# Holding back the first weight loads of the second block until a late row gather has landed

## Time and profile before

| | us |
|---|---|
| runs, not profiled | 2386.42, 2394.18, 2394.52; median 2394.18 |
| profiled execution, its own time | 2388.13 |
| its span | 2386.2 |
| PE, DVE, ACT, POOL busy | 1805.4, 1295.7, 840.0, 653.5 |
| moved by DMA | 933.05 MB, 391 GB/s over the span |

### The profile page before, as it was taken

One profiled execution on the slowest core, in us unless ns is written; L12 is line 12 of the kernel. 1 busy time (PEld: TensorE's weight loads), 2 busy tenths in 40 slices (PEclk: granted clock), 3 DMA queues, 4 the chain that ended last, 5 costly groups with the idle time before them and its releaser, 6 DMA issues.

```text
span 2386.2 us, 30584 instructions
## 1 busy us (share of the span) xinstructions
PE 1805.4 (76%) x11098; PEld 848.8 (36%) x11098; DVE 1295.7 (54%) x3184; ACT 840.0 (35%) x2262; POOL 653.5 (27%) x604
## 2 busy tenths in 40 slices
PE   6999777686787777687779557777669996766676
PEld 3654612151252343153336113333336552222222
DVE  4868777668746766856876867455424321111111
ACT  1224354434445544444744435333323410000000
POOL 1002244434433433433443444333320300000000
PEclk9999876696698888689979678877879988787878
DMA  9984999999999999999999999999986369999999
GB/s 393 376 344 194 369 422 421 421 420 420 403 421 421 420 421 420 419 390 420 420 416 421 421 420 421 421 418 419 422 328 238 140 274 428 428 428 429 428 429 378
DMA packets 110284, 933.05 MB, mean 391 GB/s; under 512 B 12710, under 2 KB 14020, under 8 KB 16644
## 3 DMA queue, kind: packets, MB, share of 16 engines
q0 software_dynamic: 76800, 549.70, 56.0%
q1 hardware_dynamic: 33348, 381.60, 38.6%
HBM read 930.15 MB, written 6.06 MB: 392 GB/s over the span
## 4 chain that ended last, share of the span: by engine, by line
DMA 50%; PE 31%; DVE 9%; ACT 6%; issue 3%; POOL 1%; SPq 0%; DVEq 0%; POOLq 0%
DMA arena<-in_peer_uv_dram,arena 28%; DMA arena<-in_moe_pieces_dram 15%; PE summed L1354 6%; DVE y_g L2781 4%; DMA mod<-in_w_parts_dram 4%; PE gp L962 3%; PE gp L1427 3%; PE gp L981 2%; DMA arena<-in_w_parts_dram 2%; PE gp L1717 2%; PE gp L972 2%; PE gp L1423 1%; PE gp L1556 1%; ACT arena L2054 1%; DMA arena<-in_w_slots_dram 1%
## 5 line engine op out<-in xcount | busy, mean ns | idle before, releaser
L1354 PE MATMUL summed<-arena 64*64 64x512 f32 x4096 | 694.6, 777 | 360.5 <-ACT arena L2054 336.5
L2781 DVE CUSTOM_DVE_ANT_0 y_g<-arena,h 128x1024 f32<-128x1024 f32 x512 | 627.1, 1225 | 459.5 <-DMA arena<-in_peer_uv_dram,arena 386.6
L902 POOL DMA_INDIRECT arena<-in_peer_uv_dram,arena x512 | 589.7, 1152 | 926.7 <-PE summed L1354 825.9
L1354 PEld LDWEIGHTS summed<-arena 64*64 64x64 f32 x4096 | 133.7, 157 | 796.8 <-ACT arena L2054 704.4
L2048 ACT ACTIVATE arena<-arena 128x1 f32<-128x1 f32 x512 | 102.7, 201 | 602.1 <-DVE arena L2781 601.4
L1717 PE MATMUL gp<-arena,mod 128*32 128x512 f32 x1008 | 164.3, 788 | 105.1 <-DMA arena<-in_moe_pieces_dram 105.1
L2054 ACT ACTIVATE arena<-cst,arena 128x128 f32<-128x128 f32 x512 | 205.5, 401 | 16.7
L3164 DVE TENSOR_TENSOR mod<-mod,gp 128x512 f32<-128x512 f32 x8 | 5.5, 688 | 367.5 <-ACT mod L2319 367.5
L2051 ACT ACTIVATE arena<-arena 128x1 f32<-128x1 f32 x512 | 150.7, 294 | 16.6
L1717 PEld LDWEIGHTS gp<-arena,mod 128*32 128x32 f32 x1008 | 32.1, 128 | 229.0 <-DMA arena<-in_moe_pieces_dram 170.4
L2319 ACT ACTIVATE mod<-gp 128x512 f32<-128x512 f32 x8 | 4.8, 597 | 261.2 <-PE gp L1717 261.2
(11 more groups left out here) (466 smaller groups left out, 2203.0 us busy)
## 6 DMA issues: line engine op xcount, KB each, us to landing
arena<-in_moe_pieces_dram SPq DMA_DIRECT2D x95, 2048.0 KB, 25.5
arena<-in_w_slots_dram SPq DMA_DIRECT2D x47, 2048.0 KB, 11.5
arena<-in_w_parts_dram SPq DMA_DIRECT2D x45, 1024.0 KB, 9.5
mod<-in_w_parts_dram SPq DMA_DIRECT2D x29, 1024.0 KB
arena<-in_peer_uv_dram,arena POOLq DMA_INDIRECT x512, 16.1
t_rep<-t_rows POOLq DMA_DIRECT2D x1, 3066.0 KB, 14.0
arena<-t_rep POOLq DMA_DIRECT2D x1, 2304.0 KB, 10.6
y_g<-in_moe_pieces_dram SPq DMA_DIRECT2D x1, 2048.0 KB, 18.1
```

The lines of the kernel that those rows point to most:

```text
L902: pool.indirect_dma_start(rowbuf[b], None, a["peer_uv"].rearrange("l n d -> (l n) d"), bass.IndirectOffsetOnAxis(ap=idx[:, col(n):col(n) + ...
L1354: mm = pe.matmul(op[o:o + HALF, b, :], diag[i:i + HALF, n % DIAGS, i:i + HALF], rowbuf[n % ROWS][i:i + HALF, D + b * 512:D + (b + 1) * 512 ...
L2781: v.tensor_tensor_reduce(y[:, t, :], rowbuf[n % ROWS][:, 0:D], h[:, t, :], 1.0, 0.0, ALU.mult, ALU.add, dots[:, c:c + 1]).then_inc(udot, 1)
```

## The change

Two lines in SP's program: before the first of the four loads at L753, SP waits until the gather of pick 509 has landed (`near = PICKS - 3 = 509`, buffer 509 % 8 = 5, and `landed(509)` is 16 * 64 = 1024, the 64th gather into that buffer). The waits on `vsum` stay.

```diff
@@ -748,6 +748,8 @@
                 sync.wait_ge(d_mm, q - 1)
                 sync.dma_start(ring2[q % 2], a["w_parts"][WQ1 + PARTS + 2 + i]).then_inc(w1_in[q % 2], 16)
 
+            near = PICKS - 3
+            sync.wait_ge(row_in[near % ROWS], landed(near))
             for n in range(phase_slots["in2"][0], phase_slots["in2"][0] + RING):
                 sync.wait_ge(vsum, rows_left(place[n]))
                 sync.dma_start(ring[:, place[n], :], a["w_slots"][n]).then_inc(w_landed[place[n]], 16)
```

## The result

The changed kernel takes 2396.04 us (median of 19 runs, 2388.39 to 2400.79), the kernel before 2389.97 (19 runs, 2384.02 to 2395.11). The ratio is 1.0024, with a 95% interval of 1.0015 to 1.0033: 5.7 us slower (the medians lie 6.1 apart). A second series of 12 runs gave 1.0011 (1.0000 to 1.0021). The forecast was 7.7 us faster. The two groups of times that I saw in four executions of the kernel before are not there in 19: they fill the range, and their median lies 4.2 us under the 2394.18 from which I reckoned.

What follows compares the result with a forecast made beforehand. It took the last gathers' landing, delayed by one DMA engine alternating gather rows with load lines, to bound the kernel. The earlier landing gives 7.7 us, the other steps nothing: from 2394.18 to 2386, range 2377 to 2394.

Steps and rivals of the forecast that it cites:

- step 5: Bias tables in the projection: at most 4.9 us later in relation to the rest, 3.0 us slack left, no cost.
- Step 1: SP's wait ends when gather 509 lands, at 1745.7; the first load moves 3.6 us later.
- Steps 2 and 3: End of picks: loads slow gather rows only 3.6 us after issue; 511's dot product at 1753.8, gain 7.7 us.
- rival A: End of picks: the 3.6 us lag doesn't carry over; with zero lag the gain is 1.0 us, 2393.2; chance 0.12.
- C: End of picks: both last gathers already inside the engine, 511 at 1750.7, gain 10.8 us, 2383.4; chance 0.13.
- Rival B: End of picks: the engine takes turns of a whole gather; gain 5.9 us, 2388.3; chance 0.07.
- Step 4: Later slot loads into the projection: first landed by 1755.5, fourth by 1770.3, all before PE needs them, no cost.
- Rival D: After the picks: bias tables or a slot come late by as much as is gained; no change, 2394; chance 0.08.
- Step 6: TensorE's clock at the last picks: may stay high, 0.9 us not counted; otherwise rises well ahead of the projection.
- Rival E: Projection: TensorE's clock low after an idle gap, costing 8.5 us, 2395.0; chance 0.04.
- The rival that ends slower: Low TensorE clock inside the projection, costing 8.5 us, 2395.0; chance 0.04.

Runs made afterwards that it cites:

- e_tables: Changed kernel plus a second SP wait, for the bias tables, before the fifth slot load; ratio 0.9957 against the kernel before.
- e_last_tables: Changed kernel with its wait on pick 511 instead of 509, plus a wait for the bias tables before the fifth slot load; ratio 0.9963.
- e_last_sixth: Changed kernel with its wait on pick 511 instead of 509, plus a wait for the bias tables before the sixth slot load; ratio 0.9955.
- e_before_split: Kernel before, no new wait, all ten slot loads of the second block as two DMAs each with 8 KB lines; ratio 0.9985.

## Why the prediction was wrong

The step that failed is **step 5**, "the bias tables, cost nothing ... at most 4.9 us later in relation to the rest and leaves 3.0 us". By it the mask should have started at 1797.2 - 1745.8 = 51.4 us after 509; it started at 64.1 and 66.2. I counted the lines that would be queued when the tables are issued, that is the fourth slot, and stopped there. The slots behind it, which SP issues at L728 while the tables are still on the engines, I left out, and with them the rule that I had worked out myself from the gathers: one packet for one line. Each load among the table packets costs them 6.0 to 6.5 us, not 4.9 once. In the kernel before, some 80 table packets were left when the fifth slot came; some 450 in the changed one. With the head start given back (e_tables) the mask starts at 40.3 and the loss is gone.

The base was off too. I took 2394.18 for the kernel before, and 19 runs give 2389.97. This hid 4.2 us of the error: the forecast, 2386, is 10.0 us from the measured 2396.04, while the change itself was forecast at -7.7 and came out at about +6.

Point by point:

- *Step 1, when the wait ends:* right. SP's first load and 509's dot product both start at 1750.36.
- *Steps 2 and 3, the lag of 3.6 us and the new landing:* right. I forecast 8.0 us from 509 to 511 and the traces show 7.4; gain 8.3 instead of 7.7. A lag of no length (rival A) and a landing at full pace (C) are out: 510 was free of delay, 511 was delayed by 2.5 us. Rival B would have 9.8 us. Whether the lag is a time or a number of rows already taken in, these gathers can't tell; the tables speak for a time (last section).
- *Step 4, the later loads:* right for this change, no slot was waited for. The first load landed 10.8 us after 509 where I had 9.7, the fourth 27.5 where I had 24.5. In e_last_tables, with less cover, one was.
- *Step 5:* wrong, as said. Rival D, "small packets behind long lines may cost more than I count", is the mechanism that happened. I gave it 0.08 and let it cost no more than the gain; it cost more, and turned the sign.
- *Step 6, the clock:* I looked for its cost ahead of the projection. It came behind the wait in the middle of it, 2.7 us. Rival E is out: the granted clock was 1.00 at the start of the projection (1770 to 1775), and in e_last_sixth PE idles for 1.55 us ahead of the turn and the clock holds. My reading of the clock before was slightly off: by windows of 0.2 and 0.5 us it fell at about 1750.55 and rose at about 1767.6, not 1750.8 and 1767.7, which changes nothing.
- *The rival that ends slower* was the wrong mechanism. Rows 12 held the right one: a wait of 26.26 us for the tables on DVE, in front of work that TensorE needs, with a slack of 7.9 us. A gain of 7.7 us upstream uses up nearly all of such a slack, unless what is waited for moves up by as much.

The rule by which e_before_split was forecast holds at the gathers to 0.3 us, so the part on which the change was built is sound; the kernel is slower for a resource that the change handed on to the next stage.

## What to carry to other kernels

A load that is held back doesn't vanish: it moves into the stretch behind, and whoever used that stretch may be late next. Before holding a transfer back, list every transfer issued in the stretch that it moves into, those in another queue too, and count packets, not bytes: here a copy of many small packets that shared the engines with long lines advanced one packet per line. Where several transfers compete, order them by when they are needed (here gathers, first slots, tables, later slots), which took a second wait of one line and gave 0.9957 where the first alone gave 1.0011 in the same series and 1.0024 in the longer one.

## What the runs showed of the hardware

- Two queues on one DMA engine took turns row by row, as the counts and times have it (the trace doesn't name the engine): 16 rows of 8 KB beside lines of 16 KB took 15.7 us, beside lines of 8 KB 9.6 us. The Trainium skill, "DMA: Bandwidth & Descriptors", section on queues, rings and completion order, has turns of whole packets of 9 to 17 descriptors; eight rows of a gather in one turn would have made 511 come at 9.8 us after 509 in the changed kernel, and it came at 7.4.
- Small packets lose more by that than rows do. Between 1786 and 1790 a table packet took 0.10 us (4 * 16 * 0.107 / 66) and its turn's line 0.83; at the gathers it was 0.31 and 0.61. The slowest table copy took 13.2 us with no slot load beside it and 19.7, 25.7 and 36.9 us with one, two and all.
- On an engine with rows waiting, the first line of a load came only some 3.6 us after the load's issue, behind about 12 rows. The forecast of 511's landing from it was 0.6 us off. At the tables the fifth slot's first lines came some 4 us after its issue (1782.15 to 1786 before; 1778.42 to 1782.5 after), while q0 moved 22 to 25 packets per engine (352 and 404 in all). So it was nearer to a fixed time than to a fixed number of packets.
